# Weighted expert sums for four slots in a row instead of two, in a kernel for a hybrid decoder layer with product-key expert retrieval

## What is computed

```python
def peer_ffn(x, wq, k1, k2, u_tab, v_tab):
    q = (x @ wq).reshape(n, 8, 2, 128)                 # 8 heads
    v1, i1 = top_k(q[:, :, 0] . k1, 16)
    v2, i2 = top_k(q[:, :, 1] . k2, 16)
    sc, pos = top_k(v1[..., :, None] + v2[..., None, :], 16)
    e = i1[pos // 16] * 128 + i2[pos % 16]             # 16 of 16384 experts per head
    g = softmax(sc)
    hsel = einsum('tsd,td->ts', u_tab[e], x)           # a dot for each token and expert
    wgt = g * gelu(hsel)
    return einsum('ts,tsd->td', wgt, v_tab[e])         # weighted sum of expert rows
```

## Time and profile before

| what | value |
|---|---|
| median of 3 runs | 1734.12 us (1733.38 to 1738.78) |
| the profiled execution | 1734.5 us, its span 1732.7 us |
| busy, share of the span | PE 71%, DVE 72%, POOL 53%, ACT 40% |
| mean granted TensorE clock | 0.84 of 2.4 GHz |
| moved by DMA | 602.42 MB, mean 348 GB/s |
| gathers | 520 indirect issues, 545 MB |
| chain that ended last | DMA 39%, PE 27%, DVE 15%, POOL 6%, ACT 5% |

### The profile page before, as it was taken

How to read it: one execution, slowest core, us unless ns; L and a number is a source line. 1 busy time by engine, 2 the same in 40 slices (tenths; PEclk the granted TensorE clock), 3 DMA queues, 4 the chain that set the end, 5 groups by cost and what they waited for, 6 DMA issues and landing times.

```text
span 1732.7 us, 19380 instructions
## 1 busy us (share of the span) xinstructions
PE 1232.9 (71%) x5360; PEld 619.5 (36%) x5360; DVE 1241.3 (72%) x2955; ACT 698.0 (40%) x1986; POOL 910.8 (53%) x1134
## 2 busy tenths in 40 slices
PE   5997898567777767767976767675766667666555
PEld 4886766322333333322322323232322222222110
DVE  3568755688887877768586778676767777767774
ACT  3321113455444444334345445343433343434444
POOL 0155120467576566555366656555656655656762
PEclk9999899778899898878986778778888887768878
DMA  6321147999999999999799999999999999999996
GB/s 173 122 98 49 37 137 100 318 390 418 414 415 416 407 418 419 417 417 398 255 388 417 419 417 416 417 378 418 419 417 418 418 418 412 409 417 402 420 415 255
DMA packets 110636, 602.42 MB, mean 348 GB/s; under 512 B 24752, under 2 KB 27184, under 8 KB 43968
## 3 DMA queue, kind: packets, MB, share of 16 engines
q0 software_dynamic: 74880, 545.29, 76.8%
q1 hardware_dynamic: 35648, 55.90, 11.0%
HBM read 597.96 MB, written 3.19 MB: 347 GB/s over the span
## 4 chain that ended last, share of the span: by engine, by line
DMA 39%; PE 27%; DVE 15%; POOL 6%; ACT 5%; issue 5%; DVEq 3%; POOLq 0%; SPq 0%; ACTq 0%
DMA arena<-in_uv,arena 38%; PE ps L985 10%; DVE arena L1848 8%; PE ps L553 5%; POOL arena L2072 4%; DVE arena L1320 3%; DVEq L1317 3%; PE ps L600 2%; POOL arena L2071 2%; PE ps L906 2%; PE ps L591 2%; DVE arena L1326 2%; PE ps L613 1%; PE ps L925 1%; ACT arena L1284 1%
## 5 line engine op out<-in xcount | busy, mean ns | idle before, releaser
L985 PE MATMUL ps<-arena 128*64 128x512 f32 x2048 | 662.8, 782 | 407.9 <-ACT arena L1284 407.7
L1848 DVE CUSTOM_DVE_ANT_0 arena<-arena 128x1024 f32<-128x1024 f32 x520 | 641.0, 1234 | 303.8 <-DMA arena<-in_uv,arena 285.0
L2072 POOL DMA_INDIRECT arena<-in_uv,arena x520 | 622.7, 1198 | 90.5 <-POOL arena L2071 8.7
L2071 POOL TENSOR_TENSOR arena<-arena 1x1 f32<-1x1 f32 x520 | 207.1, 398 | 534.9 <-PE ps L985 404.8
L985 PEld LDWEIGHTS ps<-arena 128*64 128x64 f32 x2048 | 152.1, 166 | 798.2 <-ACT arena L1284 553.2
L1278 ACT ACTIVATE arena<-arena 128x1 f32<-128x1 f32 x520 | 105.3, 202 | 757.3 <-DVE arena L1848 755.8
L1284 ACT ACTIVATE arena<-arena 128x64 f32<-128x64 f32 (+1 forms) x520 | 181.5, 349 | 17.0
L1280 ACT ACTIVATE arena<-arena 128x1 f32<-128x1 f32 x520 | 153.2, 295 | 16.9
L1320 DVE TENSOR_TENSOR arena<-arena 128x512 f32<-128x512 f32 (+7 forms) x310 | 132.6, 429 | 28.1 <-ACT arena L1032 18.9
L553 PE MATMUL ps<-arena 128*128 128x264 f32 (+1 forms) x608 | 141.9, 389 | 0.7 <-DVE arena L1320 0.7
L906 PEld LDWEIGHTS ps<-arena 128*128 128x128 f32 x1024 | 121.9, 198 | 34.9 <-issue 33.4
(11 more groups left out here) (161 smaller groups left out, 973.8 us busy)
## 6 DMA issues: line engine op xcount, KB each, us to landing
arena<-in_win SPq DMA_DIRECT2D x38, 512.0 KB, 3.3
arena<-in_wqk SPq DMA_DIRECT2D x64, 256.0 KB, 7.5
arena<-in_uv,arena POOLq DMA_INDIRECT x520, 12.3
arena<-in_wout SPq DMA_DIRECT2D x16, 512.0 KB, 7.8
arena<-in_xp SPq DMA_DIRECT2D x4, 512.0 KB, 7.5
arena<-in_wqk SPq DMA_DIRECT2D x16, 128.0 KB, 9.5
out_yp<-arena SPq DMA_DIRECT2D x4, 512.0 KB
arena<-in_const SPq DMA_DIRECT2D x1, 928.0 KB, 4.5
```

The lines of the kernel that those rows point to most:

```text
L985: last = mm(ps[64 * q:64 * q + 64, b + c, :], diag[:, (s + q) % 8, :], ring[:, (s + q) % RING, D + 512 * c:D + 512 * c + 512], start=(s == ...
L1848: v.tensor_tensor_reduce(out=ring[:, s % RING, 0:D], in0=ring[:, s % RING, 0:D], in1=row, scale=1.0, scalar=0.0, op0=MUL, op1=ADD, accum_o ...
L2071: pool.tensor_tensor(carrier[:, 1:2], carrier[:, 0:1], carrier[:, 0:1], ALU.add).then_inc(S["carried"], 1)
L2072: pool.indirect_dma_start(out=ring[:, s % RING, :], out_offset=None, in_=a["uv"][:, :], in_offset=bass.IndirectOffsetOnAxis(ap=idx[:, t, s ...
```

## The change

TensorE's loop takes four slots at a time. It waits for the fourth diagonal of the group, makes the four slots' matmuls on column half 0 and then the four on half 1 (which count `slot_used` up one by one), and only then calls `prepare` and the due mixer steps for the four slots in turn. The accumulation flags are written so that they still start with the first pair and stop with the last pair of a unit. Nothing else changes: ring, diagonals, order of accumulation for each token, the other engines' programs.

```diff
-                for s in range(0, TOPK, 2):
-                    pe.wait_ge(S["diag_done"], TOPK * u + s + 2)
+                for s in range(0, TOPK, 4):
+                    pe.wait_ge(S["diag_done"], TOPK * u + s + 4)
                     for c in range(2):
-                        for q in range(2):
-                            last = mm(ps[64 * q:64 * q + 64, b + c, :], diag[:, (s + q) % 8, :],
+                        for q in range(4):
+                            half = slice(64 * (q % 2), 64 * (q % 2) + 64)
+                            last = mm(ps[half, b + c, :], diag[:, (s + q) % 8, :],
                                       ring[:, (s + q) % RING, D + 512 * c:D + 512 * c + 512],
-                                      start=(s == 0 and u in FIRST_OF), stop=(s == TOPK - 2 and u in LAST_OF))
+                                      start=(s + q < 2 and u in FIRST_OF), stop=(s + q >= TOPK - 2 and u in LAST_OF))
                             if c:
                                 last.then_inc(S["slot_used"], 1)
-                    for q in range(2):
+                    for q in range(4):
                         if u + LEAD < NU:
                             prepare(u + LEAD, s + q)
                         later.until(pace(TOPK * u + s + q + PE_AHEAD))
```

## The result

The changed kernel takes 1932.62 us (median of 4 runs, 1932.0 to 1936.23) beside 1735.74 us for the kernel before (now the median of 4 runs too): a ratio of 1.1138, 95% interval 1.1121 to 1.1155. It is slower by 197 us. The forecast had the sign right and the size half: 1835 us, range 1765 to 1905. The profiled execution's span is 1930.5 us, 198 us above the 1732.7 of before.

What follows compares the result with a forecast made beforehand. The prediction took the stream of gathers to bound the kernel, fed by freed ring slots. Its terms, 40 + 26 + 29 + 5 + 0 = 100 us, on the profiled 1734.5 us gave 1835 us, range 1765 to 1905.

Steps and rivals of the forecast that it cites:

- 5.2 + 0.4 = 5.6 us: Group of four: three quarters of its matmuls done after 5.2 us, then 0.4 us from freeing a slot to issue.
- D: Rival: only some groups start slow (40%), 53 us lost, 1787 us; no own chance, the forecast including it has 0.74.
- The 4.7 us at the low level: PE's matmuls of a group: the first 4.7 us run at 1.2 GHz, the rest at the high clock.
- shortest landing: Last part of the ring's turn: a gather needs 5.6 us from issue to landing, leaving 6.7 us reserve below the median.
- the restart's 1.0: Gather queue run dry: landings 3.5 us apart instead of 2.5 on restart; 0.4 of that 1.0 us added per turn.
- (1): Expert units from 880 us: the ring's loop takes 20.9 us, 0.9 to 1.0 over; 40 us, bounds 0 and 87.
- (2): Eight sampled units: the samples' query and score delay the third group by 3.2 us each; 26 us, bounds 6 and 33.
- (3): 330 to 810 us, beside the second mixer half: late slots and later PE steps; 29 us, bounds 0 and 60.
- rival B: DVE starved by late PE steps in the mixer stage, each restart at full cost; 215 us, 1950 us, chance 0.12.
- (4): 806 to 870 us, PE-bound projections: same PE work, two steps in a row the rule; 5 us, bounds -5 and 15.
- (5): Key loads, end semaphore traffic, last 8 sample slots, additions into x, and all before 330 us: 0 us each.
- 418 GB/s with a median landing above 8 us: Sign, after 1200 us, for the rival that the reserve is enough: 1734 us, to 1740 with samples' delays; chance 0.11.

Runs made afterwards that it cites:

- run 1: Kernel before with only the moved steps: matmuls still by twos, queries, scores and mixer steps at every fourth slot; 1757.51 us, ratio 1.0114.
- run 2: Changed kernel with a group's matmuls made pair by pair behind the one wait for the fourth diagonal; 1873.74 us, ratio 1.0792.
- run 3: Kernel before with POOL issuing a gather only once the slot six places back is free, two buffers idle; 1868.52 us, ratio 1.0767.
- run 5: Changed kernel with four thrown-away matmuls behind the second, third and fourth group of each unit from unit 15 on; 1927.12 us, ratio 1.111.
- run 7: Kernel before with one buffer of the ring idle, POOL held back accordingly; 1754.33 us, ratio 1.0097.
- run 6: Changed kernel with ScalarE's copy of the query moved from behind slot 5 to behind slot 7; 1924.99 us, ratio 1.1098.
- run 4: Changed kernel with PE two slots more ahead in its mixer steps (PE_AHEAD 5 instead of 3); 1912.17 us, ratio 1.1027.

## Why the prediction came out at half the size

**What was right.** The sign, the bound (the stream of gathers, fed by freed slots) and the order of the parts: runs 1 to 3 show that the loss comes from freeing late. The matmuls of a group were priced well: 5.2 + 0.4 = 5.6 us from PE's start to the issue were expected, 5.40 us is the mean of the 63 groups of slots 244 to 495. "I let each group start at 1.2 GHz" is borne out by the row at 1296.39: a group behind 6.93 us of idle time takes 6.38 us, between the 3.82 us of the high clock and twice 3.68; of the 63 groups 57 took 5.0 to 6.7 us and six 3.65. So D, by which only four groups in ten start slow, is out. The Trainium skill's rule in "TensorE: Matmul & The Clock Gate", section "HAM oscillation", describes that case, and the trace agrees with it; run 5 shows that here the clock is worth little. The 4.7 us at the low level that the sum took follow from no row: in the stall read for it PE had been at the low level through the samples' query of 7.00 us too, ahead of the pair and the score. They make a whole group 6.2 us, and the mean of the 63 is 5.60.

**The step that failed: the "shortest landing" of 5.6 us as what a gather needs.** A turn in the changed kernel, mean of those 63 groups from the timeline, against the terms of the prediction: four dots of a group 8.28 us (expected 7.5), dot to diagonal 2.40 (2.2), wait for PE 0.06, start to issue 5.40 (5.6), issue to dot **7.40 (5.6)**; together 23.5 us for 8 slots, expected 20.9. The sum held its 20.9 against 19.9 (8 x 2.49); in the trace a turn of the kernel before takes 21.1 us in the mean, as key loads and stalls are in it, so the loss is 2.4 us per turn. The 5.6 us of the earlier trace rows are of gathers that met an empty queue (none other was under way at 866.8). What matters is how many are under way. From the landings of the 288 gathers of slots 208 to 495, gather by gather, in run 3 (two buffers idle) and in the kernel before:

| others under way at the issue | median issue to landing | mean distance from the landing before | gathers |
|---|---|---|---|
| 1 (run 3) | 6.9 us | 4.03 us | 8 |
| 2 (run 3) | 8.0 us | 3.05 us | 115 |
| 3 (run 3) | 9.4 us | 2.66 us | 151 |
| 4 (before) | 12.2 us | 2.65 us | 162 |
| 5 (before) | 13.5 us | 2.61 us | 106 |

(The distances hold the share of the key loads; their medians, in the table's order, are 4.08, 2.90, 2.50, 2.49 and 2.49 us. The 14 gathers of run 3 and 20 of before with other numbers are left out.) With three others under way the stream keeps its pace; with two it loses 0.4 us per gather, with one 1.4, long before the queue is dry. So the reserve was not 12.3 - 5.6 = 6.7 us but, as an estimate, 12.3 - 9.4 = 2.9 us; run 7 (2.5 us less cost 17 us) and run 3 (5 us less cost 132) bracket it. Run 3's own turn says the same, as the mean of the 126 pairs of slots 244 to 495: partner's dot 2.68, dot to diagonal 2.18, wait for PE 0.27, start to issue 3.66, issue to dot **8.36**, together 17.2 us for 6 slots. With 5.6 us in the last place it would be 14.4, inside the 14.9 that keep the pace. That a thin queue lands its gathers at a wider distance is measured; why it does stays open. My reason for adding only 0.4 us of the restart's 1.0 ("as the queue is dry only briefly") was the same mistake: the loss begins before the queue is dry.
It is also part of why runs 5 and 6 gave back so little: a gather that is issued earlier meets more others under way. In run 6 1.3 of the 1.6 us gained at the issue went into a longer way from issue to dot, in run 5 0.3 of 1.1.

**Term by term.** (1) and (2) together, slots 208 to the end: 66 us expected, 94.5 measured (87.2 + 7.3). The landing, 1.8 us longer per turn than taken, is more than this difference; the turn of 21.1 us in the kernel before, where the sum had 19.9, works against it. Within that, the samples' units were priced too high: the eight units that hold the samples' query lost 5.6 us each in the mean, the eight beside them 3.9, so 1.7 us is theirs, not 3.2. The 7.0 us of the earlier trace rows was a query at the low clock, and an outlier already in the kernel before, where the other seven took 3.7 to 4.7 us. Behind a group all eight take 3.74, here one in the changed kernel:

```profile
1167.21 3.65 PE L986 MATMUL ps<-arena 128*64 128x512 f32 x16 [3.02 <-ACT arena L1285]
1170.79 3.74 PE L925 MATMUL ps<-arena 128*128 128x8 f32 x32
```

(3), slots 12 to 176: 29 us expected, bounds 0 and 60, 71 measured. The bound was wrong as well: it was made from term 1's price. Two things add up here. With pairs freed in time it is 7 us (run 1), with pair-by-pair freeing 53 (run 2), with earlier steps 54 (run 4). The waits of this stage, first before (381 to 755 us), then after (386 to 830 us; who waits for whom, total us, times, longest):

```profile
DVE arena L1848 <- DMA arena<-in_uv,arena: 45.9, 53, 2.2
```
```profile
DVE arena L1849 <- DMA arena<-in_uv,arena: 78.6, 73, 5.5
...
DVE arena L1321 <- PE ps L613: 30.0, 9, 8.3
ACT arena L1232 <- PE ps L906: 25.1, 7, 5.3
```

33 us more of waiting for gathers, and 30 us for PE's mixer steps. The second is the mechanism of rival B, seen at its plainest at the start of a unit, where group, query and steps form one clump:

```profile
586.54 6.32 PE L986 MATMUL ps<-arena 128*64 128x512 f32 x16 [6.05 <-ACT arena L1285]
...
592.79 3.84 PE L906 MATMUL ps<-arena 128*128 128x128 f32 x32
...
596.47 1.95 PE L613 MATMUL ps<-arena 128*128 128x128 f32 x16
...
597.56 1.29 DVE L1321 TENSOR_TENSOR arena<-arena,ps 128x512 f32<-128x512 f32 x2 [8.33 <-PE ps L613]
598.98 1.23 DVE L1849 CUSTOM_DVE_ANT_0 arena<-arena 128x1024 f32<-128x1024 f32 x1
```

DVE stands 8.33 us for the step at 596.47, and the dot at 598.98 comes 12.18 us behind the one before it. The clump is PE's 6.32 + 3.84 + 1.95 us. I had counted the query for ScalarE's copy but not in front of the mixer steps. B's price for such stalls, 44 us in this stage, was nearer (30 us); its loop price behind (138 us) was too high, and its sign, that these waits outweigh those for gathers, didn't come (30.0 against 78.6 us).

(4), the projections: 5 us expected, bounds -5 and 15, 23 measured. "The same PE work stays" failed as a reason for so little: the ring runs dry behind two projection steps in a row, and then PE waits for diagonals. Changed kernel:

```profile
940.45 5.17 PE L986 MATMUL ps<-arena 128*64 128x512 f32 x16 [5.62 <-ACT arena L1285]
945.54 13.90 PE L600 MATMUL ps<-arena 128*8 128x512 f32 x32
...
963.61 5.35 PE L986 MATMUL ps<-arena 128*64 128x512 f32 x16 [3.58 <-ACT arena L1285]
```

Half of this is the moved steps by themselves (112 us in run 1), the rest comes with the grouping.
The zeros of (5) can't be told apart one by one; what could have hidden there, 3.6 us before the first dot and 5.5 in the first 12 slots, is small, and the first dot's time differs by as much among the runs (319.7 to 326.9 us).

The signs to watch, given beforehand, pointed the right way but were read with the wrong scale: the median landing fell to 9.0 us, where 7 or less was expected, at 367 GB/s, lower than the 395 expected. "418 GB/s with a median landing above 8 us" was to speak for no change. A median of 9.0 went with a loss of 11%. Two more signs came: POOL's one long wait for PE (6.82 us at 1301.86) and a lower granted clock (0.81 instead of 0.84). One did not: DVE was to wait 3 us or more for the score in the sampled units, and its waits for the score are 4.9 us in all, over 5 times, as the changed kernel's line 1758 (1757 of before) has it.

```profile
  PE ps L915: 4.9, 5
```

## What to carry to other kernels

A queue's reserve is not the median time to landing less the shortest one ever seen; ask how many transfers are under way when the next is issued, and how the distance between landings depends on that number. It is cheaply measured by holding the issuing engine back by one or two buffers, which moves nothing else. Whoever batches the consumers of a ring, to save waits that cost nothing, lengthens the hold of the first buffer by the whole batch: in a ring of eight, batches of four took the reserve, and moving other work behind the batch made clumps that hit the engines waiting for it.

## What the runs showed of the hardware that was not expected

In these runs a stream of 1 MB indirect gathers keeps its pace of one landing per 2.49 us where three or more others are under way at the issue (median distance 2.50 us at three); at two and one it slows to 2.90 and 4.08 us. The DMA share hides this: at a share of 0.95 the changed kernel moved 367 GB/s, at 1.01 the kernel before moved 417, so 6% less per busy time. The 16 increments of a landing show the thin queue as well: between the first and the last of one gather lie 4.1 us in the kernel before (slots 244 to 495, mean) and 2.1 us in run 3. As 4.1 us is more than the 2.49 us from one landing to the next, some DMA engines run more than a gather ahead of the slowest when the queue is full; that the lead is what keeps the slowest supplied is my reading; no run here tests it.
